# Feed-forward by one level of Strassen's scheme, with the squared hidden values passed through DRAM

## The chip, the cores and the metric

One core of a Trainium2 chip. The metric is the device time of one execution of the whole program in microseconds. Engines: TensorE (PE), VectorE (DVE), ScalarE (ACT), GpSimd (Pool), SyncE (SP, which here issues all DMAs). Fp32 data are multiplied as an upper part (rounded, type fp32r) and a lower part (the rest), three matmuls for each product of two tiles: lower x upper, upper x lower, upper x upper.

## The reference, cut to what matters

Two blocks of two layers each over x of 1024 rows (tokens) by 1024 columns: retention, latent attention, gated linear attention, and then the feed-forward that is changed here.

```python
D_FF = 4 * D_MODEL                       # 4096

def rms_norm(x, g):
    xf = x.astype(jnp.float32)
    y = xf * lax.rsqrt(jnp.mean(xf * xf, axis=-1, keepdims=True) + EPS)
    return (y * g.astype(jnp.float32)).astype(x.dtype)

def sqrelu_mlp(h, w1, w2):
    return jnp.square(jax.nn.relu(h @ w1)) @ w2
...
        x = x + sqrelu_mlp(rms_norm(x, norm_ffn), w1, w2)
    return rms_norm(x, final_norm)
```

In this program there is one such layer (DEPTH_2 = 1): x + mlp, then the final norm.

## The kernel before

The program is one stream per engine, with semaphores between them. Up to the gated linear attention nothing of it is changed. Two functions matter.

`gla_closing` (L3036) is the output product of the gated linear attention, in eight token tiles of 128 rows: 48 matmuls each (`multiply`), and 8 transposes of the gate product and 8 of the normalized residual (`transpose_x`, L3277). For tile t, DVE adds the residual (`finish`, L3208), ACT squares with a row sum (L3147), Pool forms 1/rms (L3188, L3190), DVE scales (`scale_x`, L3215), PE transposes, ACT copies the upper part (L3152), DVE subtracts for the lower part (L3219). The result is `x_upper` and `x_lower`, [128, 8, 1024] each, that is X transposed. These steps for tile t-1 lie in the stream beside the matmuls of tile t. The stages share `staging`, a buffer of two 128x1024 halves, and a function `later` puts the feed-forward's first loads and weight splits into the closing's loop. The last tile's transposes stand behind the feed-forward's first group.

`feed_forward` (L3325) runs over 8 chunks of 512 hidden columns. Chunk 0 is written out, chunks 1 to 6 are a hardware loop, chunk 7 is written out. In a chunk, `inner` (L3545) makes eight groups of 24 matmuls (8 k-tiles x 3), each the hidden values of 128 hidden columns by 512 tokens in one PSUM bank; ACT takes relu (L3424), DVE multiplies it with the value in PSUM (L3485), ACT copies the upper part to SBUF (L3429), DVE subtracts the lower (L3492). `outer` (L3561) then makes eight token tiles of 24 matmuls (4 k-tiles x 2 column halves x 3) into a pair of banks, and DVE adds each pair to an accumulator in SBUF (L3499). The accumulators start as the residual, loaded from DRAM (L3380). Weights come as 512 KB loads (L3360) through `staging`, are scaled with the norm's gain and split into upper (ACT, L3401, L3404) and lower (DVE, L3467, L3471). Pool has nothing to do here but the final norm's small operations. At the end each token tile is squared, scaled (L3504, L3529) and stored.

Of the kernel before, what the change touches and what calls it, by code (L numbers as in the profile page):

```python
# [2083 lines left out]
Closing = collections.namedtuple("Closing", "meanwhile programs split wl_done gT_mm gl_done y_mm y_done xl_done xn_done x_out")  # L2084
# [951 lines left out]
def gla_closing(place, sems, banks, xT, w, gain, x, ident, neghalf, staging, arrived, x_next, gated, gl, wb):  # L3036
# [5 lines left out]
    xh, xl = xT  # L3042
# [10 lines left out]
    xn = place("wc_xn", [P, DM], F32, 168 * KB)  # L3053
    SMALL = 198 * KB + 512 + 192
# [90 lines left out]
    def square_x(act, t):  # L3145
        act.wait_ge(y_done, t + 1)
        act.activation(xl[:, :, t * P:(t + 1) * P], y[:, t % 2, :].rearrange("p (k n) -> p k n", k=KT), ACT.Square,  # L3147
                       accum_out=sx[:, t % 2:t % 2 + 1]).then_inc(sx_done, 1)

    def x_upper(act, t, half):  # L3150
        act.wait_ge(xT_mm, 2 * t + half + 1)
        act.activation(xh[:, 4 * half:4 * half + 4, t * P:(t + 1) * P],  # L3152
                       x_ps[half][:, :].rearrange("p (k n) -> p k n", k=4), ACT.Copy).then_inc(xh_done, 1)
# [18 lines left out]
    def scalar(act, later):  # L3172
        for t in range(1, NT):
# [3 lines left out]
            later(act, t)  # L3177
            for half in range(2):
                x_upper(act, t - 1, half)
            if t + 1 < NT:  # L3180
                g_upper(act, t + 1, 1)
        square_x(act, NT - 1)

    def gpsimd(pool):
        for t in range(NT):
            u = t % 2
            pool.wait_ge(sx_done, t + 1)
            pool.tensor_scalar(mx[:, u:u + 1], sx[:, u:u + 1], 1.0 / DM, EPS, ALU.mult, ALU.add).then_inc(mx_done, 1)  # L3188
            pool.wait_ge(mx_done, t + 1)
            pool.tensor_tensor(rx[:, u:u + 1], mx[:, u:u + 1], neghalf[:], ALU.pow).then_inc(rx_done, 1)  # L3190

# [19 lines left out]
    def scale_x(dve, t):  # L3211
# [28 lines left out]
    def vector(dve, later):  # L3240
        for t in range(1, NT):
# [74 lines left out]
    def last_x(pe):  # L3316
        for half in range(2):
# [3 lines left out]
                   (sync, scalar, gpsimd, vector, tensor), (x_upper, x_lower, last_x),  # L3321
                   wl_done, gT_mm, gl_done, y_mm, y_done, xl_done, xn_done, x_out)


def feed_forward(place, sems, banks, x, xT, gain, w1, w2, g_final, neghalf, staging, arrived, out, gl, wc):  # L3325
# [4 lines left out]
    FT = HALF // P  # L3330
    xh, xl = xT
    f_ps, y_ps = banks
    w1h = [place(f"ff_w1h{n}", [P, 2, HALF], F32R, at * KB) for n, at in enumerate((72, 76, 128, 148))]
    w1l = [place(f"ff_w1l{n}", [P, 2, HALF], F32R, at * KB) for n, at in enumerate((160, 192, 144, 152))]
    hh = place("ff_hh", [P, FT, SEQ], F32R, 80 * KB)
    hl = place("ff_hl", [P, FT, SEQ], F32R, 96 * KB)
    w2h = [place(f"ff_w2h{f}", [P, DM], F32R, at * KB) for f, at in enumerate((136, 180, 64, 132))]
    w2l = [place(f"ff_w2l{f}", [P, DM], F32R, at * KB) for f, at in enumerate((140, 184, 68, 188))]
    acc = [place(f"ff_acc{t}", [P, DM], F32, at * KB) for t, at in enumerate((156, 164, 112, 116, 120, 124, 172, 176))]
    relu = place("ff_relu", [P, HALF], F32, 196 * KB)  # L3340
    SMALL = 198 * KB
    ss, ms, rms = (place("ff_" + n, [P, NT + 1], F32, SMALL + 64 * i) for i, n in enumerate(("ss", "ms", "rms")))
    raw = staging

    def sem(name):
        return sems("ff_" + name)

    raw_in = arrived
    (x_in, final_in, out_done, ss_done, ms_done, rms_done, wh_done,
     wl_done, f_mm, relu_done, sq_done, hh_done, hl_done, y_mm, y_added, fin_done) = (  # L3350
        sem(n) for n in ("x_in final_in out_done ss_done ms_done rms_done "
                         "wh_done wl_done f_mm relu_done sq_done hh_done hl_done y_mm y_added fin_done").split())
    END = NC - 1

    def load_w(sp, c, n):
        if n < 4:
            src = w1[ds(c, 1), :, 2 * n:2 * n + 2, :].rearrange("a p k n -> p (a k n)")
        else:
            src = w2[ds(c * HALF + (n - 4) * P, P), :]
        sp.dma_start(raw[:, n % 2, :], src).then_inc(raw_in[n % 2], 16)  # L3360

    def sync_later(sp, t):
        if t == 0:
            sp.wait_ge(wc.wl_done, 7)
            load_w(sp, 0, 0)
            sp.wait_ge(wc.wl_done, 8)
            load_w(sp, 0, 1)
        if t in (4, 5):
            sp.wait_ge(wl_done, t - 3)
            load_w(sp, 0, t - 2)  # L3370

    def sync(sp):
        for n in range(4, 8):
            sp.wait_ge(wl_done, n - 1)
            load_w(sp, 0, n)
        for slot in range(2):
            sp.wait_ge(wc.x_out[slot], 16 * NT // 2)
        sp.wait_ge(wc.xn_done, NT)
        for t in range(NT):
            sp.dma_start(acc[t][:, :], x[t * P:(t + 1) * P, :]).then_inc(x_in, 16)  # L3380
        with sp.Fori(1, NC) as c:
            for n in range(8):
# [393 lines left out]
```

## Time and profile before

| | before |
|---|---|
| median of 3 runs | 2540.96 us (2540.87 to 2540.98) |
| span of the profiled execution | 2538.1 us |
| PE busy | 2511.3 us, 99% |
| DVE, ACT, Pool busy | 1239.0, 923.3, 461.0 us |
| feed-forward, from its first matmul to its last | 1834.1 to 2531.7 us |
| DMA, whole run | 194.34 MB, mean 77 GB/s |

The profile is of one execution; times are from the span's start. "Busy" of PE is not its rate: matmuls are pipelined and overlap in the record. An engine's idle time counts only where the end hangs on it. "L" is a line of the kernel before.

### The profile page before, as it was taken

What the parts mean: (1) busy time and instruction counts of PE and PEld (TensorE: products, weight loads), DVE (VectorE), ACT (ScalarE), POOL (GpSimd) and SP (SyncE); (2) the same over time, 40 slices, a digit from 0 to 9 for tenths busy, and PEclk for the clock granted to TensorE, in tenths of its full rate; (3) what the DMA queues carried; (4) which work ended last, traced back from release to release, by engine and by line L of the source; (5) the groups of instructions that cost most, each with busy time, mean ns of one, the idle gap of its engine ahead of it and who ended that gap; (6) DMA issues with size and microseconds to landing.
All of it is one profiled execution on the core that took longest, in us unless ns stands there. A gap on an engine that the chain in (4) does not pass through costs nothing.

```text
span 2538.1 us, 34788 instructions
## 1 busy us (share of the span) xinstructions
PE 2511.3 (99%) x12376; PEld 2113.7 (83%) x12376; DVE 1239.0 (49%) x2573; ACT 923.3 (36%) x1848; POOL 461.0 (18%) x933
## 2 busy tenths in 40 slices
PE   8999999999999999999899999999999999999998
PEld 7888888888888988888788888888888888888887
DVE  4553634535423521577755867865443333333334
ACT  5443433424313423555544544443332122112212
POOL 3453533435000304422000000110000000000001
PEclk9999999999999999999999999999999999999999
DMA  5220311202532222222242111113331111111111
GB/s 213 79 77 20 93 39 55 68 19 92 205 116 92 80 87 65 57 60 61 98 160 100 40 62 45 48 63 126 112 132 37 47 58 50 41 50 58 36 48 75
DMA packets 76396, 194.34 MB, mean 77 GB/s; under 512 B 8560, under 2 KB 29424, under 8 KB 75504
## 3 DMA queue, kind: packets, MB, share of 16 engines
q1 hardware_dynamic: 76272, 192.69, 23.1%
q8 instruction: 77, 1.26, 0.2%
q14 instruction: 47, 0.39, 0.0%
HBM read 152.29 MB, written 36.18 MB: 74 GB/s over the span
## 4 chain that ended last, share of the span: by engine, by line
PE 95%; DVE 2%; DMA 1%; ACT 1%; issue 1%; SPq 0%; POOL 0%; DVEq 0%; POOLq 0%; ACTq 0%
PE wc_g_ps L3545 14%; PE wc_y_ps L3561 14%; PE ra_qkv_ps L1245 14%; PE gl_vr_ps L2676 7%; PE wa_y_ps L365 7%; PE ra_gate_ps L1245 7%; PE gl_j_ps L2635 3%; PE la_x_ps L1478 3%; PE wb_y_ps L3009 3%; PE wc_y_ps L3294 3%; PE la_cq_ps L1400 1%; PE la_kv_ps L1400 1%; PE at_T_ps L1967 1%; PE gl_l_ps L2702 1%; PE at_j_ps L1918 1%; PE at_v_ps L1918 1%
## 5 line engine op out<-in xcount | busy, mean ns | idle before, releaser
L3545 PE MATMUL wc_g_ps<-x_upper,ff_w1l 128*128 128x512 f32 x512 | 199.3, 389 | 0.0
L3545 PE MATMUL wc_g_ps<-x_upper,ff_w1h 128*128 128x512 f32 x512 | 199.2, 389 | 0.0
L3561 PE MATMUL wc_y_ps<-ff_w2l,ff_hh 128*128 128x512 f32 x512 | 199.2, 389 | 0.0
L3545 PE MATMUL wc_g_ps<-x_lower,ff_w1h 128*128 128x512 f32 x512 | 199.2, 389 | 0.0
L3561 PE MATMUL wc_y_ps<-ff_w2h,ff_hl 128*128 128x512 f32 x512 | 199.2, 389 | 0.0
L3561 PE MATMUL wc_y_ps<-ff_w2h,ff_hh 128*128 128x512 f32 x512 | 199.2, 389 | 0.0
L3499 DVE TENSOR_TENSOR ff_acc<-wc_y_ps,ff_acc 128x1024 f32<-128x1024 f32 x63 | 77.2, 1225 | 210.8 <-PE wc_y_ps L3561 210.8
L3424 ACT ACTIVATE ff_relu<-wc_g_ps 128x512 f32<-128x512 f32 x64 | 38.3, 599 | 378.9 <-PE wc_g_ps L3545 378.9
L3485 DVE SCALAR_TENSOR_TENSOR wc_g_ps<-wc_g_ps,ff_relu 128x512 f32<-128x512 f32 x64 | 44.8, 700 | 178.6 <-ACT ff_relu L3424 178.6
L3453 POOL TENSOR_SCALAR ff_ms<-ff_ss 128x1 f32<-128x1 f32 x8 | 1.8, 221 | 686.9 <-ACT x_lower L3441 686.0
L3545 PEld LDWEIGHTS wc_g_ps<-x_upper,ff_w1h 128*128 128x128 f32 x512 | 96.1, 188 | 20.0
L3561 PEld LDWEIGHTS wc_y_ps<-ff_w2h,ff_hh 128*128 128x128 f32 x512 | 96.1, 188 | 20.0
L3561 PEld LDWEIGHTS wc_y_ps<-ff_w2l,ff_hh 128*128 128x128 f32 x512 | 96.1, 188 | 20.0
L3545 PEld LDWEIGHTS wc_g_ps<-x_lower,ff_w1h 128*128 128x128 f32 x512 | 96.1, 188 | 20.0
L3561 PEld LDWEIGHTS wc_y_ps<-ff_w2h,ff_hl 128*128 128x128 f32 x512 | 96.1, 188 | 19.9
L3545 PEld LDWEIGHTS wc_g_ps<-x_upper,ff_w1l 128*128 128x128 f32 x512 | 96.1, 188 | 19.9
L1245 PE MATMUL ra_qkv_ps<-ra_wide_h,ra_xl 128*128 128x512 f32 x256 | 104.1, 407 | 8.5 <-DVE ra_wide_l L975 8.2
L1030 DVE TENSOR_TENSOR ra_sT<-ra_s_ps,ra_decay 128x128 f32<-128x128 f32 x64 | 18.6, 291 | 188.4 <-PE ra_s_ps L1284 188.4
L1245 PE MATMUL ra_qkv_ps<-ra_narrow_h,ra_xl 128*128 128x512 f32 x256 | 103.7, 405 | 0.0
L365 PE MATMUL wa_y_ps<-wa_wh,wa_gl 128*128 128x512 f32 x256 | 102.2, 399 | 0.8 <-DVE ra_vl L1050 0.6
L2676 PE MATMUL gl_vr_ps<-gl_vrh,x_lower 128*128 128x512 f32 x256 | 102.1, 399 | 0.0
L1245 PE MATMUL ra_qkv_ps<-ra_wide_h,ra_xh 128*128 128x512 f32 x256 | 101.0, 395 | 0.0
(460 smaller groups left out, 6995.0 us busy)
## 6 DMA issues: line engine op xcount, KB each, us to landing
staging<-in_w_ff SPq DMA_DIRECT2D x64, 512.0 KB, 3.7
ra_raw<-in_w_wide_a SPq DMA_DIRECT2D x24, 512.0 KB, 3.9
ra_raw<-in_w_narrow_a SPq DMA_DIRECT2D x16, 512.0 KB, 3.7
staging<-in_w_vr_c SPq DMA_DIRECT2D x16, 512.0 KB, 4.5
wa_gin<-gated_a SPq DMA_DIRECT2D x6, 1024.0 KB, 4.8
ra_first_raw<-in_w_wide_a SPq DMA_DIRECT2D x8, 512.0 KB, 8.1
ra_x_rows<-in_x SPq DMA_DIRECT2D x8, 512.0 KB, 5.7
gated_a<-ra_sg SPq DMA_DIRECT2D x32, 128.0 KB, 2.0
```

Source lines behind the costliest of these rows:

```text
L365: last = pe.matmul(y_ps[slot][:, c, :], a[:, slot, kt, :], b[kt][:, c * HALF:(c + 1) * HALF], start=(kt == 0 and i == 0), stop=(kt == KW - ...
L1245: last = pe.matmul(out, a[:, kt, t * P:(t + 1) * P], b[:, kt, at:at + HALF], start=(kt == 0 and i == 0), stop=(kt == KT - 1 and i == 2))
L1400: last = pe.matmul(out, xx[kt // 4][:, kt % 4, t * P:(t + 1) * P], ww[:, kt, a:b], start=(kt == 0 and i == 0), stop=(kt == KT - 1 and i == 2))
L1478: last = pe.matmul(x_ps[:, j % 2, :], a[:, kt, f % 4 * P:(f % 4 + 1) * P], b[kt // 4][:, kt % 4, half * HALF:(half + 1) * HALF], start=(kt ...
L1918: pe.matmul(out, al, bh, start=start, stop=False)
L2635: last = pe.matmul(out, w[:, r, cols], xx[:, r, at], start=(r == 0 and i == 0), stop=(r == KT - 1 and i == 2))
L2676: last = pe.matmul(vr_ps[t % 2][:, :], xx[:, r, t * P:(t + 1) * P], w[:, r, :], start=(r == 0 and i == 0), stop=(r == KT - 1 and i == 2))
L3009: last = pe.matmul(y_ps[t % 2][:, c, :], a[t % 2][:, kt, :], b[kt][:, c * HALF:(c + 1) * HALF], start=(kt == 0 and i == 0), stop=(kt == KW ...
L3294: last = pe.matmul(y_ps[t % 2][:, c, :], a[t % 2][:, kt, :], b[kt][:, c * HALF:(c + 1) * HALF], start=(kt == 0 and i == 0), stop=(kt == KW ...
L3499: dve.tensor_tensor(acc[t][:, :], y_ps[t % 2][:, :, :].rearrange("p a n -> p (a n)"), acc[t][:, :], ALU.add).then_inc(y_added, 1)
L3545: last = pe.matmul(f_ps[j % 2][:, :], a[kt // 2][:, kt % 2, f * P:(f + 1) * P], b[:, kt, half * HALF:(half + 1) * HALF], start=(kt == 0 an ...
L3561: last = pe.matmul(y_ps[t % 2][:, n, :], a[:, f, t * P:(t + 1) * P], b[f][:, n * HALF:(n + 1) * HALF], start=(f == 0 and i == 0), stop=(f ...
```

## The change

X (tokens by features) and W1 are each cut into 2 x 2 blocks: tokens into even and odd tiles of 128, features into two halves; a chunk of 512 hidden columns into two halves of 256. One level of Strassen's scheme (Winograd's form) gives the four result blocks by 7 block products in place of 8. The same is done for the second product over the chunk (hidden by output columns). Products are chained in PSUM: three open a bank pair (start=True), the other four add to a pair that stands, and between them the state is copied or added out.

- Eight banks are four pairs. First product: the 7 products use pair0, pair1, pair2, pair0, pair0, pair0, pair2; `snap` (ACT, 512 wide) copies pair0 after products 1, 4, 5 and 6; `add_square` (DVE) adds pair1 or pair2 to three of these and squares with relu; `square` does the fourth. The four squared blocks of a chunk are stored to a DRAM tensor `hidden` (8 x 4 x 128 x 1024 fp32).
- All first products of the 8 chunks run first, then all second products, which load `hidden` and W2 again, four blocks of 512 KB each and chunk.
- Weight factors: four differences of blocks on Pool per chunk (`difference_first`, `_second`, `_last`), upper part on ACT, lower on DVE, in a ring of three, two products ahead. X factors: in `gla_closing`, per pair of tiles, sums on DVE and Pool (`s1`, `s2_sum`, `s3_sum`); `s4_sum` in two 2048-wide Pool operations and the split of s2 and s4 inside the first chunk. The norm's gain moves from the weights to the scaling of X (`scale_x` with `row`).
- Second product, chunks 0 to 6: both factors of a product are split: 14 upper parts on ACT, 10 lower on DVE, 4 on Pool, and Pool makes 8 sums. Every product of 24 matmuls is two pairs, and DVE adds each pair (128x1024) to an accumulator: 14 `evict` a chunk, where before there were 8 adds. Chunk 7 is done in the plain form (`direct`).
- The hardware loop is gone: the feed-forward is written out. Semaphores of the attention are cleared (by Pool) and reused.

The diff, cut to its core:

```diff
     def scale_x(dve, t):
-        dve.tensor_scalar(xn[:, :], y[:, t % 2, :], rx[:, t % 2:t % 2 + 1], None, ALU.mult).then_inc(xn_done, 1)
+        dve.scalar_tensor_tensor(xn[:, :], y[:, t % 2, :], rx[:, t % 2:t % 2 + 1], row[:, :],
+                                 ALU.mult, ALU.mult).then_inc(xn_done, 1)
...
     def scalar(act, later):
-            later(act, t)
...
+            x_upper(act, t - 1)
             if t + 1 < NT:
                 g_upper(act, t + 1, 1)
+            if t % 2 == 0:
+                sum_upper(act, t // 2 - 1)
+        later(act)
         square_x(act, NT - 1)
...
+    def scalar_later(act):
+        act.wait_ge(wc.cleared, 1)
+        w_upper(act, 0, 0)
+        w_upper(act, 0, 1)
...
+    def gpsimd(pool):
+        sums(pool, NT // 2 - 1)
+        difference_second(pool, 0)
...
+        pool.tensor_tensor(gathered(xf.s4_sum), gathered(xf.a12[0]).bitcast(F32), xf.s2_sum[:, :, :, :],
+                           ALU.subtract).then_inc(wc.xs_done, 1)
+        pool.wait_ge(wc.xs_done, 9)
+        pool.tensor_tensor(xf.s4_sum[:, :, :], xf.s4_sum[:, :, :], xf.a12[1][:, :, :].bitcast(F32), ALU.add).then_inc(wc.xs_done, 1)
+        difference_last(pool, 0)
+        for c in range(1, NC):
+            difference_first(pool, c)
+            difference_second(pool, c)
+            difference_last(pool, c)
+        sums_first(pool, 0)
+        sums_second(pool, 0)
+        second_lower(pool, 0, 1, 1, True)
+        for c in range(END):
+            sums_last(pool, c)
+            for p in (3, 4):
+                for side in range(2):
+                    second_lower(pool, c, p, side, True)
+            if c + 1 < END:
+                sums_first(pool, c + 1)
+                sums_second(pool, c + 1)
...
+    POOL_LOWER = ((4,), (1, 3, 4))
...
+    def vector(dve):
+        w_lower(dve, 0, 1)
+        scale_x(dve, NT - 1)
+        split(dve, xf.s3[1][:, :, early], xf.s3_sum[:, :, early], xf.s3[0][:, :, early], 1)
+        w_lower(dve, 0, 2)
+        x_lower(dve, NT - 1)
+        split(dve, xf.s3[1][:, :, 3 * P:], xf.s3_sum[:, :, 3 * P:], xf.s3[0][:, :, 3 * P:], 2)
+        sum_lower(dve, NT // 2 - 1)
+        for c in range(NC):
+            for p in range(PRODUCTS):
+                if c == 0 and p == 0:
+                    continue
+                if c == 0 and p == 1:
+                    add_square(dve, c, p)
+                    split(dve, gathered(xf.s2[1]), xf.s2_sum[:, :, :, :], gathered(xf.s2[0]), 3)
+                ahead = PRODUCTS * c + p + 2
+                if ahead < PRODUCTS * NC:
+                    w_lower(dve, *divmod(ahead, PRODUCTS))
...
+        for c in range(END):
+            for p in range(PRODUCTS):
+                n = PRODUCTS * c + p
+                if n:
+                    evict(dve, *divmod(n - 1, PRODUCTS), 1)
+                ahead = divmod(n + 2, PRODUCTS)
+                second_lower(dve, *ahead, 0, False)
+                evict(dve, c, p, 0)
+                second_lower(dve, *ahead, 1, False)
...
+        def inner(c, p):
+            bank = (pair0, pair1, pair2, pair0, pair0, pair0, pair2)[p]
+            pe.wait_ge(wl_done, n + 1)
...
+            for j in range(2):
+                if p in (3, 4, 5):
+                    pe.wait_ge(snap_done, 8 * c + {3: 0, 4: 2, 5: 4}[p] + j + 1)
...
+                for kt in range(KT // 2):
+                    for i, (a, b) in enumerate(((lower, xh), (upper, xl), (upper, xh))):
+                        last = pe.matmul(bank[:, j, :], a[:, kt, j * P:(j + 1) * P], b[:, kt, :],
+                                         start=(p < 3 and kt == 0 and i == 0), stop=(kt == KT // 2 - 1 and i == 2), skip_group_check=p > 2)
...
+        def outer(c, p):
+            for pair in range(2):
+                own = p in (0, 3, 4, 5)
+                bank = ((pair1, pair3) if own else (pair0, pair2))[pair]
+                last = {2: 2, 3: 0, 4: 6, 5: 8, 6: 4}.get(p)
+                if last is not None:
+                    pe.wait_ge(ev_done, 14 * c + last + pair + 1)
```

## Rows read from the trace of the kernel before

**Rows 1.** Page: span, PE's busy time, and the chain's shares by engine.

```profile
span 2538.1 us, 34788 instructions
PE 2511.3 (99%) x12376; PEld 2113.7 (83%) x12376; DVE 1239.0 (49%) x2573; ACT 923.3 (36%) x1848; POOL 461.0 (18%) x933
...
PE 95%; DVE 2%; DMA 1%; ACT 1%; issue 1%; SPq 0%; POOL 0%; DVEq 0%; POOLq 0%; ACTq 0%
```

**Rows 2.** Stretches: limits, length, busy us (instructions), clock, DMA share, GB/s.

```profile
1834.10:1878.70 44.60, 44.60 (x202) 37.02 (x201) 18.03 (x23) 14.25 (x22) 0.74 (x2) 1.00 0.44 166
1878.70:1922.20 43.50, 43.50 (x193) 36.02 (x192) 15.26 (x17) 6.32 (x10) 0.00 (x0) 1.00 0.19 61
1922.20:2009.30 87.10, 87.10 (x386) 72.09 (x386) 31.13 (x36) 18.50 (x28) 0.00 (x0) 1.00 0.15 49
```

**Rows 3.** Groups by line and shape: busy us, mean ns | idle before, releaser.

```profile
L3499 DVE TENSOR_TENSOR ff_acc<-wc_y_ps,ff_acc 128x1024 f32<-128x1024 f32 x63 | 77.2, 1225 | 210.8 <-PE wc_y_ps L3561 210.8
L3429 ACT ACTIVATE ff_hh<-wc_g_ps 128x512 fp32r<-128x512 f32 x64 | 38.4, 600 | 48.3 <-DVE wc_g_ps L3485 48.3
L3471 DVE TENSOR_TENSOR ff_w2l<-staging,ff_w2h 128x1024 fp32r<-128x1024 f32 x32 | 39.2, 1226 | 7.9 <-ACT ff_w2h L3404 7.9
L3404 ACT ACTIVATE ff_w2h<-staging 128x1024 fp32r<-128x1024 f32 x32 | 33.7, 1052 | 0.0
L3504 DVE SCALAR_TENSOR_TENSOR ff_acc<-ff_acc,ff_rms,staging 128x1024 f32<-128x1024 f32 x7 | 8.9, 1279 | 0.0
L3523 DVE TENSOR_TENSOR ff_acc<-wc_y_ps,ff_acc 128x512 f32<-128x512 f32 x2 | 1.4, 692 | 1.1 <-PE wc_y_ps L3561 1.1
...
L1786 POOL TENSOR_TENSOR at_rl<-at_twice,at_rh 128x512 fp32r<-128x512 f32 x15 | 19.3, 1284 | 86.8 <-ACT at_rh L1676 86.8
L1780 POOL TENSOR_TENSOR gate_lower<-at_v,gate_upper 128x1024 fp32r<-128x1024 f32 x8 | 19.2, 2403 | 38.3 <-ACT gate_upper L1667 38.3
```

**Rows 4.** Timeline, first token tile's end: start us, duration us, engine, line.

```profile
1884.17 0.39 PE L3561 MATMUL wc_y_ps<-ff_w2h,ff_hl 128*128 128x512 f32 x1
...
1884.37 1.23 DVE L3499 TENSOR_TENSOR ff_acc<-wc_y_ps,ff_acc 128x1024 f32<-128x1024 f32 x1 [2.75 <-PE wc_y_ps L3561]
```

**Rows 5.** DMA issues (us to landing), and SP's timeline.

```profile
ff_acc<-x SPq DMA_DIRECT2D x8, 512.0 KB, 7.2
...
1856.37 3.93 SPq L3380 DMA_DIRECT2D ff_acc<-x  x8
```

**Rows 6.** Timeline of DVE and Pool in retention; then one line's min/median/max ns.

```profile
303.58 0.45 POOL L873 TENSOR_TENSOR ra_rot<-ra_qk,ra_cos 128x128 f32<-128x128 f32 x1 [2.44 <-ACT ra_qk L665]
303.62 0.70 DVE L998 TENSOR_TENSOR staging<-ra_oS,staging 128x256 f32<-128x256 f32 x1
303.99 0.64 POOL L874 TENSOR_TENSOR ra_rot<-ra_qk,ra_cos 128x128 f32<-128x128 f32 x1
...
L998 DVE TENSOR_TENSOR ra_sg<-ra_oS,ra_sg x32: 424/427/718, 51.1 to 592.7; 128x256 f32<-128x256 f32 x32
```

**Rows 7.** Timeline of DVE and Pool in attention.

```profile
1039.42 2.40 POOL L1780 TENSOR_TENSOR gate_lower<-at_v,gate_upper 128x1024 fp32r<-128x1024 f32 x1 [2.02 <-ACT gate_upper L1667]
...
1039.64 0.42 DVE L1855 TENSOR_TENSOR gate_lower<-at_T_ps,gate_upper 128x256 fp32r<-128x256 f32 x1
...
1040.55 1.48 DVE L1864 TENSOR_SCALAR at_prob<-at_prob,at_rinv 128x384 f32<-128x384 f32 x1
...
1044.66 0.49 DVE L1864 TENSOR_SCALAR at_prob<-at_prob,at_rinv 128x512 f32<-128x512 f32 x1
```

**Rows 8.** Timeline where the feed-forward begins (first matmul 1834.1 us).

```profile
1833.11 0.60 ACT L3152 ACTIVATE x_upper<-wc_x_ps 128x512 fp32r<-128x512 f32 x1 [2.61 <-PE wc_x_ps L3277]
...
1834.55 1.23 DVE L3208 TENSOR_TENSOR wc_y<-wc_y_ps,wc_xin 128x1024 f32<-128x1024 f32 x1
...
1837.90 0.75 DVE L3215 TENSOR_SCALAR wc_xn<-wc_y,wc_rx 128x1024 f32<-128x1024 f32 x1 [2.13 <-POOL wc_rx L3190]
...
1839.74 1.03 PE L3277 MATMUL wc_x_ps<-ident,wc_xn 128*128 128x128 f32 x8
```

More of the change, by code:

```diff
@@ L3328, in feed_forward @@
+def feed_forward(place, sems, banks, x, xf, w1, w2, g_final, neghalf, staging, hidden, out, gl, wc):
     KB = 1024
     NC = D_FF // HALF
[L3330 to L3340, printed above, removed]
+    END = NC - 1
+    PRODUCTS = 7
+    x_upper, sum_upper, sums, scale_x, x_lower, sum_lower, last_x = wc.split
+    B11, B12, B21, B22 = range(4)
@@ L3372, in sync @@
[L3372 to L3386 removed]
+            sp.wait_ge(wc.cleared, 1)
@@ new lines, in second_lower, with late_lower @@
+    def second_lower(eng, c, p, side, mine):
+        done, count = lowered(side, c, p)
+        if (p in POOL_LOWER[side]) != mine:
+            return
+        n = PRODUCTS * c + p
+        upper, lower = slots[n % 3][2 * side:2 * side + 2]
+        eng.wait_ge((ph_done, qh_done)[side], n + 1)
+        eng.tensor_tensor(lower[:, :, :], second(c, p)[side], upper[:, :, :].bitcast(F32), ALU.subtract).then_inc(done, 1)
+    def late_lower(pool, side, blk, n):
+        pool.wait_ge(late_h, n + 1)
+        upper, lower = late[side, blk]
+        pool.tensor_tensor(lower[:, :, :], (h_raw, w_raw)[side][END % 2][blk], upper[:, :, :].bitcast(F32),
+                           ALU.subtract).then_inc(late_l, 1)
@@ L3525, in vector @@
+        for half in range(2):
+            dve.wait_ge(y_mm, NT + half)
+            dst = acc[1][:, half, t // 2, :]
+            dve.tensor_tensor(dst, y_bank(t)[:, half, :], dst, ALU.add).then_inc(y_added, 1)
             if half == 0:
@@ new lines, in outer @@
+        def outer(c, p):
+            n = PRODUCTS * c + p
+            ah, al, bh, bl = slots[n % 3]
+            for side in range(2):
+                pe.wait_ge(*lowered(side, c, p))
+            for pair in range(2):
+                own = p in (0, 3, 4, 5)
+                bank = ((pair1, pair3) if own else (pair0, pair2))[pair]
+                last = {2: 2, 3: 0, 4: 6, 5: 8, 6: 4}.get(p)
+                if last is not None:
+                    pe.wait_ge(ev_done, 14 * c + last + pair + 1)
+                elif c:
+                    pe.wait_ge(ev_done, 14 * (c - 1) + (10, 12)[p] + pair + 1)
+                elif own:
+                    if pair == 0:
+                        pe.wait_ge(add_done, 6 * END + 2)
+                elif pair == 0:
+                    pe.wait_ge(snap_done, 8 * NC)
+                else:
+                    pe.wait_ge(add_done, 6 * NC)
+                for u in range(2):
+                    i = 2 * pair + u
+                    for k in range(2):
+                        for m, (a, b) in enumerate(((al, bh), (ah, bl), (ah, bh))):
+                            end = pe.matmul(bank[:, u, :], a[:, k, i * P:(i + 1) * P], b[:, k, :],
+                                            start=(p < 3 and k == 0 and m == 0), stop=(k == 1 and m == 2), skip_group_check=p > 2)
+                end.then_inc(p_mm, 1)
@@ L3682, in build @@
             x_ps = [bank("wc_x_ps0"), bank("wc_x_ps1")]
+        with ExitStack() as third:
+            ff_banks = [third.enter_context(nc.psum_tensor(f"ff_ps{i}", [P, 2, HALF], F32)) for i in range(4)]
+        xf = x_forms(place)
         wb = attention_closing(place, sems, opening_banks, xT, t["w_out_b"], x1, t["g_post_b"], ident, neghalf, staging,
```

739 lines of the change are left out of this document (524 added, 215 removed).

## The prediction

> **What bounds the kernel now.** I read the page's head and its chain of waits first: PE carries 95% of the chain and is busy for 99% of the span, so only work taken from PE, or a wait put in front of it, moves the end [rows 1]. "Busy" here is not its pace: a 128x512 matmul is recorded with 389 ns, but the next starts earlier. The table by stretches gives the pace: the 192 matmuls of one second-product pass take 43.50 us, and two further passes (384 matmuls) 87.10 us, so one costs 0.2267 us, at a granted clock of 1.00 (2.4 GHz) [rows 2]. The first stretch in it is straight-line code with 8 transposes, the third is loop code; the pace is the same, so I charge nothing for the loops being written out. The other engines have room: in the pass at 1922.2 DVE is busy 31.1 of 87.1 us and ACT 18.5.
>
> **What is removed.** Before, a chunk of 512 hidden columns has 192 + 192 matmuls, eight chunks 3072. After, a first product is 7 products x 24 = 168 per chunk (1344), the second is 168 for seven chunks (1176), and the last chunk keeps the plain form (192): 2712. So 360 go: 360 x 0.2267 = **81.6 us**. Tile shapes stay 128x128 by 128x512.
>
> One product now is 24 x 0.2267 = 5.44 us, a half of it 2.72, a chunk of seven 38.1 us. Everything that feeds a product must fit there. Prices of one operation on 128x1024 fp32 [rows 3]: ACT copy 1.05, DVE add from PSUM 1.23, DVE subtraction with both inputs in SBUF 1.23, DVE scaled two-input form 1.28, Pool 2.40. A 512-wide ACT copy from PSUM is 0.60, a 512-wide DVE add 0.69, a 512-wide Pool operation 1.28.
>
> **First product, steady state: hidden.** Per chunk ACT has 7 copies and 8 snapshots (7.4 + 4.8 = 12.2 us), DVE 7 lower parts, 6 adds and 4 squares (8.6 + 4.1 + 5.1 = 17.8), Pool 4 differences (9.6). The new tight wait is that of the fifth product on the snapshot of the fourth, same bank pair: a half is ready 2.72 us before its half-bank is wanted, DVE starts 0.20 us after PE's boundary [rows 4], ACT about the same, and 0.60 follows: 1.9 us to spare, with the weight copy ahead of it (1.05) done by then. SP's stores of hidden blocks wait behind squares, and the next chunk's loads are queued ahead of them, so nobody waits for that. Stores and loads add 32 MB; eight 512 KB loads issued within 3.93 us landed with a median of 7.2 us [rows 5], some 15 us for a chunk's 4 MB of the second product in the worst reading, with some 25 us between the release of the buffers and their first use. I cost the trip through DRAM at nothing; without that cover it would be 5 us a chunk.
>
> **A resource shared by DVE and Pool.** In retention, a Pool operation runs from 303.58 to 304.03; a DVE operation with two SBUF inputs starts at 303.62 and takes 0.70 against 0.43 for its form in most cases; it ends 0.29 after Pool, which is its 256 elements at 1.04 ns. The next Pool operation takes 0.64, not 0.45: it ends 0.31 after DVE [rows 6]. In attention a Pool operation runs from 1039.42 to 1041.82. DVE work from PSUM beside it takes its usual 0.42 (no wait), while a 384-wide SBUF scaling takes 1.48 and ends 0.21 after Pool; a wider one that starts just ahead of a Pool operation takes 0.49 [rows 7]. So these two kinds exclude each other for their whole length and take turns; a DVE operation with one input in PSUM does not take part. Scaled to 1024 elements, DVE ends 1.09 after Pool and Pool 2.28 after DVE: a turn of both is 3.37 us. The Trainium skill (SBUF — State Buffer, section "SBUF: two separate sides") says the same as a rule: the pair of ports shared by DVE and Pool is an exclusive lock and the loser blocks for the whole instruction. It speaks against this change, which puts 4 to 12 Pool operations per chunk where there were none; without it the sum below would be that of the first rival.
>
> **Second product, steady state.** Per chunk DVE evicts 14 pairs (17.2 us) and makes 10 of the 14 lower parts (12.3): 29.4 of 38.1. Pool makes 8 sums and 4 lower parts: 28.8. Alone, each fits. But Pool's 12 and DVE's 10 two-input operations exclude each other: 12 x 2.28 + 10 x 1.09 = 38.3, just over PE's 38.1, if no turn is ever lost. And DVE is in order: eviction, lower part, eviction, lower part. In products 4 to 6 of a chunk (both lower parts on DVE, Pool busy throughout with the sums) a half costs a turn, 3.37, against 2.72: DVE falls behind 0.65 a half. PE meets this where a product writes the banks of the one before (3rd after 2nd, 5th after 4th, 6th after 5th). There an eviction has 2.72 - 0.20 - 1.23 = 1.3 us of slack. Laid out with Pool 1.1 us from the end of its operation when the 4th product begins, PE waits 0.3 + 0.6 + 0.6 there, and, as DVE carries the lag into the next chunk, 1.6 before its 3rd product: 3.1 us. With Pool just finished at that moment it is 0.45 and little after. I take 2.5 us for each of the six chunks with sums for a next one: **+15 us**. Ends: 0 and 6 a chunk (36 us). A gain is excluded, since nothing here shortens a matmul.
>
> **The entry.** (1) The opening weight copy. Before, it is done in good time; now it stands after the closing's last ACT copy for tile 6, which runs 1833.11 to 1833.71 [rows 8]. ACT 1.05, then the DVE part 1.23: the first matmul moves from 1834.1 to about 1836.1: **+2.0**. (2) The closing itself: scaling with the gain row is 1.28, where 0.75 stood [rows 3, 8], and one DVE operation is added before the residual add of every second tile: **+1.0** (0 to 2). (3) The first chunk's fourth product. It needs X-sum s2 (split on DVE, 128x2048) and its weight's lower part, which DVE does after it. In us from 1834.1: PE starts at 2.0, the second product ends at 14.0 (with 8 transposes, 1.03 [rows 8]), the third at 19.4, when the fourth wants to start. DVE: residual add until 3.1, scaling until 6.5 (it waits for the square and the power), split of s3 until 8.2, weight part until 9.4, tile 7's parts until 11.4, the rest of s3 at 12.5, the s1 part blocked by Pool's third difference until 15.3, adds until 16.6. Then Pool takes 4.64 for each of its two 2048-wide operations for s4 (1.28 for 512 and 2.40 for 1024 give 2.19 ns an element). The square waits for the first, to 21.0. The split of s2 waits for the second: 25.5, then 2.2 of its own: 27.7. The weight part waits for the last difference: 31.1. So PE waits 31.1 - 19.4 = **+11.7**. Without exclusion the same queue ends at 21.2: +1.8, the lower end; upper end 16, should a further Pool operation get in.
>
> **The seam and the tail.** From first to second product, chunk 0's hidden blocks and weights are requested in the 1st and 2nd product of the last chunk and used from the 6th, 20 us later: covered. Pool's six sums then need some 14 us before the second product's lower part, wanted at 43.5 us from that chunk's start: done by 38 to 42, covered. The last chunk and the tail keep matmuls and operations: 0.
>
> **Sum.** Against the profiled span: 2538.1 - 81.6 + 2.0 + 1.0 + 11.7 + 15.0 = 2486.2. The median of the runs is 2540.96, 2.9 above the span: **2489**.
>
> **Rivals.** (A) No exclusion that matters, because the turns fall into waits that DVE has anyway: 2540.96 - 81.6 + 2.0 + 1.8 = 2463. For it: each engine alone fits, and DVE waited 210.8 us for PE around its adds before [rows 3]. Against: the blocked operations [rows 6, 7], and Pool with 28.8 of 38.1 us. 20%. (B) The lag compounds: DVE never recovers in the products with one lower part, or the loads arrive late behind Pool's slips: 6 us a chunk, 2510. 13%. (C) Slower: evictions are excluded by Pool as well (they read and write an accumulator in SBUF). Then Pool's 28.8, and DVE's 12.3 and 17.2, run one after the other: 58.3 us a chunk, 20.2 above PE, over six chunks 121: 2540.96 - 81.6 + 14.7 + 121 = 2595. The sign turns at some 11 us a chunk. Against it is the 0.42 us operation from PSUM beside Pool [rows 7]. 4%. That the change does not do what it says (matmuls not removed) has no room: the count is in the code.
>
> **How the numbers follow.** Forecast 63%, A 20%, B 13%, C 4%. The forecast's own range is 2476 to 2502. The range of 8 in 10 takes in A's point and most of B: 2462 to 2511. 0.2% (5 us) is about what a measurement of this kernel can tell from no change. Faster than 2536: all but C and a thin end of B: 95%; within 0.2%: 1%; slower 4%.
>
> **What would show each step.** 2712 matmuls of the feed-forward at 0.2267 where PE does not wait; Pool operations with DVE's two-input operations ending 1.1 us after them and stretched beyond 1.23; DVE evictions at 1.23 whatever Pool does; a PE wait of some 12 us before the 4th product of the first chunk, ended by DVE's weight part; 1 to 3 us per chunk before the 3rd, 5th and 6th products of the second stage, ended by DVE evictions. The prediction is wrong if PE runs the second stage without waits (then A), if evictions are stretched (then C), or if the matmul pace changes.

## The result, and the profile after

The changed kernel takes **2497.26 us** (median of 4 runs, 2496.68 to 2498.04) against 2540.91 in the same rounds: ratio 0.9828 [0.9815, 0.9842], 43.7 us less. The forecast was 2489 with a range of 2462 to 2511: sign and range held, and the kernel is 8 us slower than the point. The profiled execution spans 2496.2 us, 41.9 less than that of before. The page's head and chain, as in [rows 1]:

```profile
span 2496.2 us, 34303 instructions
...
PE 2439.3 (98%) x12016; PEld 2047.3 (82%) x12016; DVE 1439.2 (58%) x2608; ACT 985.2 (39%) x1862; POOL 821.6 (33%) x1064
...
PE 84%; DVE 9%; issue 4%; DMA 1%; ACT 1%; SPq 0%; POOL 0%; DVEq 0%; POOLq 0%; ACTq 0%
```

The 360 instructions are gone from PE (12376 to 12016). PE still carries the chain, but DVE has 9% of it where it had 2%. PE's waits (line, releaser: us in total, times, longest us) say where; those of the attention are left out:

```profile
PE ff_ps L4021 <- DVE ff_even L3891: 13.2, 6, 5.9
PE ff_ps L3991 <- DVE ff_w_lower L3851: 11.3, 1, 11.3
...
PE ff_ps L3991 <- issue: 2.6, 1, 2.6
...
PE ff_ps L4021 <- DVE ff_odd L3891: 2.1, 7, 0.4
```

Line numbers of the changed kernel: L3991 is `inner`, L4021 `outer`, L3891 `evict`, L3796 the second product's lower parts, L3851 the weights' lower parts, L3855 `split`, L3860 the square, L3809 and L3812 Pool's two operations for s4, L3749 the last difference behind them. The table by stretches, in the columns of [rows 2]: first the stretch that stands second there, then the whole first product, and one steady chunk of the second.

```profile
1878.70:1922.20 43.50, 43.50 (x193) 36.03 (x192) 24.00 (x23) 13.91 (x18) 10.52 (x4) 1.00 0.28 104
...
1838.20:2157.00 318.80, 307.45 (x1351) 254.20 (x1352) 174.19 (x144) 106.06 (x133) 112.90 (x43) 0.98 0.33 122
...
2258.17:2298.32 40.15, 38.66 (x169) 31.38 (x169) 36.24 (x25) 14.07 (x15) 34.73 (x13) 1.00 0.27 105
```

The first line has the pace of before, 193 matmuls in 43.50 us. So what a stage takes beyond its count of matmuls is loss. The stages are cut at the starts of their first matmuls (1838.2, 2157.3, 2446.1); one matmul of the first product still starts behind the 2157.00 of the second line.

| stage | measured us | matmuls alone | loss | forecast |
|---|---|---|---|---|
| up to the first feed-forward matmul | 1838.2, before 1834.1 | | 4.1 | 3.0 |
| first product: 56 products, 8 transposes | 319.0 | 56 x 5.44 + 1.03 = 305.7 | 13.3 | 11.7 |
| second product: 49 products | 288.8 | 49 x 5.44 = 266.6 | 22.2 | 15.0 |
| last chunk and tail | | | 0 | 0 |

The losses sum to 39.6, and 81.6 - 39.6 = 42.0, against 41.9 between the spans.

**Before the fourth product.** DVE, Pool and PE in the timeline:

```profile
1851.08 5.05 POOL L3809 TENSOR_TENSOR xf_s_sum<-xf_a_upper,xf_s_sum 128x2048 f32<-128x2048 f32 x1
...
1852.90 4.32 DVE L3860 SCALAR_TENSOR_TENSOR ff_c<-ff_c 128x1024 f32<-128x1024 f32 x1
...
1856.20 5.36 POOL L3812 TENSOR_TENSOR xf_s_sum<-xf_s_sum,xf_a_lower 128x2048 f32<-128x2048 f32 x1
...
1857.14 6.58 DVE L3855 TENSOR_TENSOR xf_s_lower<-xf_s_sum,xf_s_upper 128x2048 fp32r<-128x2048 f32 x1
...
1861.53 4.38 POOL L3749 TENSOR_TENSOR staging<-staging,ff_t 128x1024 f32<-128x1024 f32 x1
...
1863.64 4.49 DVE L3851 TENSOR_TENSOR ff_w_lower<-ff_t,ff_w_upper 128x1024 fp32r<-128x1024 f32 x2
...
1867.05 0.80 PE L3991 MATMUL ff_ps<-xf_s_upper,ff_w_lower 128*128 128x512 f32 x1 [11.32 <-DVE ff_w_lower L3851]
```

Read the ends, not the durations. Pool's first s4 operation ends at 1856.13 and the square (1.28 alone, [rows 3]) at 1857.22, 1.09 later. Pool's second ends at 1861.56, the split 2.16 later. This is the queue that the prediction wrote down.

**The clock** was in no term of the sum. Stretches at this wait, and the same at the 5.9 us wait before the third product of the second stage's first chunk (the granted clock is the third number from the end; 0.50 is 1.2 GHz):

```profile
1865.00:1867.00 2.00, 0.00 (x0) 0.00 (x0) 2.00 (x2) 0.00 (x0) 0.91 (x1) 0.50 0.00 0
1867.00:1870.00 3.00, 2.95 (x7) 2.37 (x8) 2.26 (x2) 0.00 (x0) 1.70 (x1) 0.50 0.00 0
...
1871.00:1873.00 2.00, 2.00 (x10) 1.63 (x9) 0.00 (x0) 0.60 (x1) 1.86 (x2) 1.00 0.00 0
...
2176.00:2178.00 2.00, 2.00 (x6) 1.58 (x5) 0.00 (x0) 0.00 (x0) 1.61 (x1) 0.50 1.03 406
2178.00:2180.00 2.00, 2.00 (x10) 1.63 (x10) 0.95 (x1) 0.00 (x0) 0.00 (x0) 1.00 0.16 57
```

Behind the first wait the matmuls start 0.43 us apart instead of 0.227: ten of them take from 1867.05 to 1871.17, 4.1 us in place of 2.3. That is 1.8 us on top of the 11.3. A wait is counted from the recorded end of a matmul, 0.39 after its start, and the next could have started 0.23 after it: that makes 0.2 more, and together the 13.3 of the table.

**The steady chunk.** DVE and Pool take turns:

```profile
2268.51 3.39 POOL L3765 TENSOR_TENSOR ff_v<-ff_v,ff_v 128x1024 f32<-128x1024 f32 x1
2271.86 3.40 POOL L3767 TENSOR_TENSOR ff_a<-ff_a,ff_a 128x1024 f32<-128x1024 f32 x1
...
2270.69 2.30 DVE L3796 TENSOR_TENSOR ff_p<-ff_a,ff_p 128x1024 fp32r<-128x1024 f32 x1
2272.91 1.21 DVE L3891 TENSOR_TENSOR ff_odd<-ff_ps,ff_odd 128x1024 f32<-128x1024 f32 x1
2274.04 2.29 DVE L3796 TENSOR_TENSOR ff_p<-staging,ff_p 128x1024 fp32r<-128x1024 f32 x1
...
2258.17 38.69 PE L4021 MATMUL ff_ps<-ff_p,ff_p 128*128 128x512 f32 x168 [1.46 <-DVE ff_even L3891]
2298.32 38.68 PE L4021 MATMUL ff_ps<-ff_p,ff_p 128*128 128x512 f32 x168 [1.46 <-DVE ff_even L3891]
```

A turn is 3.35 us (forecast 3.37); a lower part begun under Pool takes 2.3 in place of 1.23, and an eviction from PSUM 1.21 whatever Pool does, so rival C falls. PE's one long wait of a chunk is before its third product: 1.46, or 1.6 against the pace. Another 0.1 is lost within that product, and 0.3 within the sixth. From the third product of one chunk to that of the next it is 40.13 to 40.15 us, 2.05 above 38.1.

**The seam.** The third product of chunk 2 starts at 2258.17. Its two chunks and two products before it are 16 x 5.44 = 87.0 us of matmuls, so without loss it would start at 2157.3 + 87.0 = 2244.3, and 13.9 us are lost by then. Two steady losses make 4.1; the other 9.8 are the entry into the second stage, where the prediction had 0.

```profile
2160.07 2.33 DVE L3860 SCALAR_TENSOR_TENSOR ff_c<-ff_c 128x1024 f32<-128x1024 f32 x1
...
2161.26 3.40 POOL L3786 TENSOR_TENSOR ff_a<-ff_a,ff_u 128x1024 f32<-128x1024 f32 x1
...
2162.32 3.42 DVE L3796 TENSOR_TENSOR ff_p<-ff_a,ff_p 128x1024 fp32r<-128x1024 f32 x1
...
2165.67 1.21 DVE L3891 TENSOR_TENSOR ff_even<-ff_ps,ff_even 128x1024 f32<-128x1024 f32 x1
...
2174.18 2.05 PE L4021 MATMUL ff_ps<-ff_p,ff_p 128*128 128x512 f32 x4 [5.88 <-DVE ff_even L3891]
```

PE closes the first product at 2157.3, and DVE still has its last sums and square to do, beside lower parts stretched by Pool. Its first eviction starts at 2165.67, though PE had filled that pair at 2157.3 + 2.72 = 2160.0. PE's third product waits for the third eviction: that pair was filled at 2165.4 and the eviction starts at 2172.83. It could have started 0.2 behind PE, so it is 7.2 us late; less its slack of 1.3 (2.72 - 0.20 - 1.21), that is the wait of 5.9.

### The profile page after: what moved, and what is told of

It reads as the page before. It is cut to its first block, busy times and chain, and to the rows that moved or that the text cites. A ratio compares the mean times of both kernels' runs of the same rounds, so it can differ in the third digit from the quotient of the medians.

```text
span 2496.2 us, 34303 instructions
## 1 busy us (share of the span) xinstructions
PE 2439.3 (98%) x12016; PEld 2047.3 (82%) x12016; DVE 1439.2 (58%) x2608; ACT 985.2 (39%) x1862; POOL 821.6 (33%) x1064
## 4 chain that ended last, share of the span: by engine, by line
PE 84%; DVE 9%; issue 4%; DMA 1%; ACT 1%; SPq 0%; POOL 0%; DVEq 0%; POOLq 0%; ACTq 0%
PE ra_qkv_ps L1252 14%; PE ff_ps L3991 11%; PE gl_vr_ps L2683 7%; PE ra_gate_ps L1252 7%; PE wa_y_ps L372 6%; PE ff_ps L4021 4%; PE la_x_ps L1485 3%; PE wb_y_ps L3016 3%; PE wc_y_ps L3394 3%; DVE ff_p L3796 3%; PE gl_j_ps L2642 3%; PE ff_ps L4051 2%; DVE ff_odd L3891 1%; PE la_cq_ps L1407 1%; DVE ff_even L3891 1%
## 5 line engine op out<-in xcount | busy, mean ns | idle before, releaser
L4021 PE MATMUL ff_ps<-ff_p,ff_p 128*128 128x512 f32 x1176 | 273.5, 393 | 15.4 <-DVE ff_even L3891 13.2
L4021 PEld LDWEIGHTS ff_ps<-ff_p,ff_p 128*128 128x128 f32 x1176 | 220.6, 189 | 68.2 <-issue 18.1
L3991 PE MATMUL ff_ps<-xf_s_upper,ff_w_lower 128*128 128x512 f32 x256 | 100.5, 392 | 11.3 <-DVE ff_w_lower L3851 11.3
L1252 PE MATMUL ra_qkv_ps<-ra_wide_l,ra_xh 128*128 128x512 f32 x256 | 100.7, 394 | 0.0
L1252 PE MATMUL ra_qkv_ps<-ra_narrow_h,ra_xh 128*128 128x512 f32 x256 | 100.3, 392 | 0.0
L3991 PE MATMUL ff_ps<-xf_s_lower,ff_w_upper 128*128 128x512 f32 x256 | 100.3, 392 | 0.0
L3991 PE MATMUL ff_ps<-xf_s_upper,ff_w_upper 128*128 128x512 f32 x256 | 100.2, 391 | 0.0
L1252 PE MATMUL ra_qkv_ps<-ra_narrow_l,ra_xh 128*128 128x512 f32 x256 | 100.1, 391 | 0.0
L1252 PE MATMUL ra_gate_ps<-ra_wide_h,ra_xl 128*128 128x512 f32 x256 | 100.1, 391 | 0.0
L372 PE MATMUL wa_y_ps<-wa_wh,wa_gh 128*128 128x512 f32 x256 | 100.0, 391 | 0.0
```

Source lines behind the costliest of these rows:

```text
L372: last = pe.matmul(y_ps[slot][:, c, :], a[:, slot, kt, :], b[kt][:, c * HALF:(c + 1) * HALF], start=(kt == 0 and i == 0), stop=(kt == KW - ...
L1252: last = pe.matmul(out, a[:, kt, t * P:(t + 1) * P], b[:, kt, at:at + HALF], start=(kt == 0 and i == 0), stop=(kt == KT - 1 and i == 2))
L3991: last = pe.matmul(bank[:, j, :], a[:, kt, j * P:(j + 1) * P], b[:, kt, :], start=(p < 3 and kt == 0 and i == 0), stop=(kt == KT // 2 - 1 ...
L4021: end = pe.matmul(bank[:, u, :], a[:, k, i * P:(i + 1) * P], b[:, k, :], start=(p < 3 and k == 0 and m == 0), stop=(k == 1 and m == 2), sk ...
```

## Experiments

All medians below are of fresh runs against the kernel before in the same rounds (2540.4 to 2540.7 there). The single edits gain little beside the spread of their runs: the ratios of `e1`, `e7` and `e4` are 0.982, 0.9818 and 0.9817 with about 0.0016 to either side, against 0.9828 [0.9815, 0.9842] for the change. Their medians alone tell none of them from the changed kernel, and those of `e1`, `e4`, `e5` and `e7` lie 1.3 to 3.1 us above what was forecast. What these edits show is read from their waits; what they are worth together is timed at the end, beside the changed kernel. Spans are of one execution, for `e4`, `e5` and `e7` the fastest of four.

**Is the wait before the fourth product Pool's s4 work?** First edit (`e1`), both s4 operations moved behind what DVE owes the fourth product, and the last difference ahead of them:

```diff
         difference_second(pool, 0)
+        difference_last(pool, 0)
+        pool.wait_ge(sl_done, 3)
+        pool.wait_ge(wl_done, 4)
         pool.wait_ge(wc.y_mm, NT)
...
-        difference_last(pool, 0)
```

> Pool makes its last difference of the first chunk first, and begins the two 2048-wide operations for s4 only when DVE has split s2 and made the fourth product's weight part; nothing else moves. Theory (DVE's two-input operations and Pool's exclude each other for their whole length): the square, the split of s2 and the weight part lose about 9 us of blocking, so PE's wait before the fourth product goes from 11.3 to 2 to 3 us, and the half-speed matmuls behind it (about 1.7 us) go as well. s4 now comes later: a new wait of 3 to 5 us before the sixth product. Net 6 to 9 us less than the changed kernel: 2488 to 2491. Rival (DVE's queue is simply too long there, whatever Pool does): DVE's operations keep 4.3, 6.6 and 3.4 us, the wait stays at 11, and s4's delay comes on top: 2497 to 2502.

Measured 2494.04 (2491.2 to 2499.0), span 2491.6.

```profile
1857.78 0.50 PE L3993 MATMUL ff_ps<-xf_s_upper,ff_w_lower 128*128 128x512 f32 x1 [2.69 <-DVE ff_w_lower L3853]
...
1873.43 0.76 PE L3993 MATMUL ff_ps<-xf_s_upper,ff_w_lower 128*128 128x512 f32 x1 [4.48 <-DVE xf_s_lower L3857]
```

The wait falls from 11.3 to 2.7, so Pool's work at that point is its cause: the two s4 operations and, by the queue above, the last difference behind them, which the edit moves too. 4.5 come back before the sixth product, which needs s4. Second edit (`e7`): only the second s4 operation and the difference behind it wait.

> Of the two 2048-wide Pool operations for s4 the first stays where it is and only the second, and the last difference behind it, wait for DVE's split of s2 and weight part. Theory (each 2048-wide Pool operation blocks DVE once, by up to 4.6 us): the square is still blocked, the split of s2 and the weight part are not: PE waits 4 to 5 us before the fourth product and nothing before the sixth, since s4 is ready by then. Its two waits are 4 to 5 us in all, against 11.3 in the changed kernel and 7.2 (2.7 + 4.5) with both operations late: 6 to 8 us less than the changed kernel, 2489 to 2491, with half-speed matmuls behind the wait as after the 4.5 us one. Rival (the wait before the fourth product is made by the chain of operations on DVE whatever order Pool has, and the 2.7 us was because Pool was quite idle): 7 us or more remain, 2493 or more.

Measured 2494.06 (2491.2 to 2496.0), span 2489.4: one wait of 4.9, and 0.7 before the sixth product. DVE's square is blocked once (4.33 us), its split no longer (2.28).

**Do Pool's sums cost the second product its 22 us?** (`e2`) The sums are left out, and raw blocks stand in as factors:

```diff
-        return (..., (u2[:, :, :], v2[:, :, :]), (u1[:, :, :], v1[:, :, :]),
+        return (..., (h[3], w[B22]), (h[2], w[B11]),
...
-            sums_last(pool, c)
...
-                sums_first(pool, c + 1)
-                sums_second(pool, c + 1)
```

> Leaves out Pool's 8 sums per chunk of the second product (the factors are the raw blocks, so the output is not the reference's); the same number of copies, lower parts, evictions and matmuls stays. Theory (exclusion): DVE's lower parts return to 1.2 us, all waits of PE in the second product go: a chunk takes 38.1 instead of 40.1 us, and the seam loses most of its 10 us: 22 us less in the second product, 2475 to 2478. Rival (DVE's own load of 29 us in 38, in order, is what PE waits for): a chunk keeps 1 to 2 us of waits before the third, fifth and sixth products, the seam keeps 5 or more: 2485 to 2495.

Measured 2478.14 (2477.5 to 2478.8, two runs). DVE still makes as many lower parts and evictions. The stretch of one chunk, and DVE's groups:

```profile
2220.00:2258.10 38.10, 38.10 (x170) 31.55 (x169) 28.48 (x25) 14.10 (x15) 9.82 (x4) 1.00 0.30 111
...
L3796 DVE TENSOR_TENSOR ff_p<-ff_a,ff_p 128x1024 fp32r<-128x1024 f32 x36 | 43.7, 1215 | 0.0
```

The second product runs from 2159.9 to 2426.5 by its matmuls' starts, 266.6 us: its count times the pace. All 22.2 us, at the seam too, hang on Pool's sums, and a lower part is back at 1215 ns.

**Does it matter when the sums come?** (`e3`) The three of `sums_second` moved behind `second_lower(c + 1, 1, 1)`:

> Pool makes the last two sums of the next chunk (v2, u2) after its lower part for the next chunk's second product, not before it, so that of the six sums in a row four remain beside products 4 to 6 of a chunk. Theory (a half-product with one turn of DVE and one of Pool costs 3.35 us against 2.72, and PE waits once the lag is over 1.3 us; only the number of such halves in a row counts): four or five in a row instead of six or seven, so the wait per chunk falls from 2.05 to 0.5 to 1.2 us: 5 to 8 us less over the chunks, 2489 to 2493. Rival (the exclusive resource is full over the whole chunk, 38.0 of 38.1 us, so order does not matter): unchanged, 2496 to 2499, the waits only move to other products.

Measured 2497.09 (2495.8 to 2499.2). A chunk takes 40.4 against 40.15; the waits only move (0.65 before the third product, and 0.7 each, by the pace, within the fifth and the sixth). The theory that a burst of sums was the cost fell.

**The shared time, or DVE's queue?** (`e9`) All lower parts on DVE. Pool's 8 sums and DVE's 14 then exclude each other for 8 x 2.28 + 14 x 1.09 = 33.5 us, below 38.1.

```diff
-    POOL_LOWER = ((4,), (1, 3, 4))
+    POOL_LOWER = ((), ())
```

> All four lower parts that Pool makes per chunk go to DVE; Pool keeps its 8 sums. Sum of turns 33.5 us a chunk, DVE's own work 28 operations: 32.2 us back to back. Theory 1 (exclusive resource full): no reason for a wait is left, 38.1 us a chunk and a shorter seam: 2478 to 2484. Theory 2 (DVE's time, with 0.9 us of blocking for each lower part that meets a sum, and a lag that grows in every half-product with a turn of both): 32.2 + 8 x 1.1 = 41 us a chunk or more: 2498 to 2508.

```profile
2256.37:2297.30 40.93, 39.04 (x168) 31.21 (x169) 40.71 (x29) 14.05 (x15) 24.91 (x8) 1.00 0.27 103
```

Measured 2502.12 (2500.7 to 2504.6). The chunk takes 40.93 us and DVE is busy for 40.71 of them: what is full here is DVE's queue, its own work plus the time it is blocked. The shared resource is not: by the timeline, Pool's sums and DVE's lower parts together cover 34.3 us of the chunk. In the changed kernel it is otherwise: Pool's operations and DVE's lower parts cover 38.7 of 40.15 us, more than the 38.1 that PE needs, and DVE is busy for 36.24. So there the shared time is all but full as well, and these runs do not separate which of the two makes its 2.05 us.

With one lower part moved to DVE (`e8`, `POOL_LOWER = ((), (1, 3, 4))`):

> One lower part per chunk of the second product (the fifth product's, hidden side) goes from Pool to DVE. Taking turns costs Pool 2.28 us and DVE 1.09, so the sum of turns falls from 38.3 to 37.1 us a chunk, while DVE's own work rises from 29.4 to 30.6. Theory 1 (the exclusive resource is what is full over a chunk, as the unchanged time with spread sums suggests): a chunk falls from 40.1 by about 1.2, to 38.9; 7 us less in all: 2489 to 2491. Theory 2 (DVE's time is full: its 24 operations at 1.15 us plus 0.9 us for each lower part that meets a Pool operation make 36 us, and one more adds 1 to 2): a chunk stays at 40.1 or rises to 41: 2496 to 2503.

Measured 2509.45 (2507.6 to 2511.1), above both forecasts and worse than all fourteen on DVE, with PE waiting on `ff_even` 12.7 us in 7 waits and on `ff_odd` 6.7 in 23. A chunk takes 42.1 us and DVE is busy for 41.6 of them, so its queue is full here too. Its eleven lower parts meet eleven operations of Pool and take 2.41 us each (1.21 to 3.26), 26.5 a chunk. In `e9` fourteen meet only eight and take 1.84 each, 25.8 a chunk: the moved part adds to DVE's work and takes off little of its blocking. Of the 7.6 us between the two spans 3.1 arise ahead of the second product, in code that both share. Why the ten parts of the changed kernel take only 2.09 each is open.

**The seam** (`e4`). Pool's last sums of chunk 0 wait until DVE's third eviction is done:

```diff
+            if c == 0:
+                second_lower(pool, c, 3, 1, True)
+                pool.wait_ge(ev_done, 3)
             sums_last(pool, c)
```

> In the first chunk of the second product Pool makes the lower part of the fourth product first and then waits until DVE has evicted three pairs before its last two sums of that chunk. Theory (the seam's 5.9 us wait comes from DVE operations of 3.4, 2.3 and 2.8 us that stand behind Pool's sums, at a moment when DVE also has the last squares of the first product to do): the wait before the third product falls to 0 to 2 us, and with it the half-speed matmuls behind it; 6 to 8 us less: 2489 to 2491. Rival (the seam is DVE's backlog of squares and adds alone, or the late loads): the wait stays at 4 us or more, 2494 to 2498, and Pool's later sums may add to it.

Measured 2493.17 (2491.3 to 2496.4).

```profile
2160.28 1.23 DVE L3863 SCALAR_TENSOR_TENSOR ff_c<-ff_c 128x1024 f32<-128x1024 f32 x1
...
2161.42 1.22 DVE L3796 TENSOR_TENSOR ff_p<-ff_a,ff_p 128x1024 fp32r<-128x1024 f32 x1
...
2162.56 1.22 DVE L3894 TENSOR_TENSOR ff_even<-ff_ps,ff_even 128x1024 f32<-128x1024 f32 x1
...
2169.97 2.32 PE L4024 MATMUL ff_ps<-ff_p,ff_p 128*128 128x512 f32 x9 [1.45 <-DVE ff_even L3894]
```

The square and the lower part are back at their own times, the first eviction starts 3.1 us sooner, and the wait falls from 5.9 to 1.45. The granted clock stays at 1.00 in the stretch 2168 to 2176. The second product takes 281.8 us in place of 288.8.

**The opening** (`e5`). The upper and the lower part of the first weight are made right behind tile 6's square and scaling, ahead of its transposes' copies (`later` moved up in both loops):

> The first weight block's upper part (ACT) and lower part (DVE) are made right after tile 6 is squared and scaled, not behind ACT's last copy of tile 6. Theory (the 2.6 us before the feed-forward's first matmul are this copy and DVE's part, which Pool's difference stretches to 2.24): PE goes on without a wait, 2 to 3 us less: 2494 to 2495. Rival (PE waits there for tile 6's own lower part or for Pool's difference): the wait stays at 2 us or more, 2496 to 2498.

Measured 2496.28 (2494.9 to 2497.8). The opening wait is gone (first matmul at 1835.9, not 1838.2), but the wait at the seam is 6.5 there. By its ratio, 0.9827 [0.981, 0.9843], the kernel alone can't be told from the change.

**Joined.** `e7`, `e4` and `e5` in one kernel (`e10`), the first two without the opening (`e12`), and the changed kernel again beside them:

> The three edits together: the second of Pool's two 2048-wide operations for s4 waits for the split of s2 and the fourth product's weight part; in the second product's chunk 0 Pool's last sums come behind one lower part and DVE's third eviction; the opening weight parts are made right behind tile 6. Theory (waits are serial on TensorE, so gains add): opening wait 2.7 less, wait before the first chunk's fourth product 11.3 to 4.9 and no matmuls at half speed behind it, wait at the seam 5.9 to about 1.5 and its half-speed matmuls gone. Against the changed kernel alone, the profiled span falls by 2.7 + 6.4 + 6.8 = 16 at most: 2480 to 2484, median 2483 to 2488. Rival (the wait removed in front comes back at the next place, since Pool's queue is one chain, as the seam's wait grew from 5.9 to 6.5 when the opening wait went): not more than the best single edit, 2490 or above.

> The same without the edit of the opening: s4's second operation later and the seam's order. Theory (gains add): the opening's wait of 2.7 us stays, the other two waits as in the run with all three; 2.7 us slower than that run, median 2486 to 2490. Rival (the opening's wait only shifts DVE and Pool together with TensorE, and is given back by the following wait): within 1 us of the run with all three.

> The changed kernel as it is, on the same chip and in the same rounds as the two joined versions, to have the difference between them without a change of chip. Both theories: 2496 to 2498 median, span about 2496, waits of 11.3, 5.9 and 2.7 us before the fourth product of the first chunk, at the seam and at the opening.

| | median us (5 runs) | ratio to before |
|---|---|---|
| changed kernel again | 2498.95 (2498.45 to 2499.72) | 0.9835 [0.9822, 0.9849] |
| s4 and seam | 2487.98 (2487.07 to 2490.65) | 0.9793 [0.978, 0.9807] |
| s4, seam and opening | **2483.79** (2483.01 to 2484.16) | 0.9775 [0.9761, 0.9788] |

PE's waits in the kernel with all three:

```profile
PE ff_ps L4028 <- DVE ff_even L3898: 8.2, 6, 1.5
PE ff_ps L3998 <- DVE ff_w_lower L3858: 5.0, 1, 5.0
...
PE ff_ps L4028 <- DVE ff_odd L3898: 1.3, 4, 0.4
```

The gains add: 15.2 us below the changed kernel on the same chip, by spans 3.0 up to the first feed-forward matmul, 5.6 in the first product, 6.9 in the second. The opening is worth 4.2 between the medians of the last two, whose runs do not overlap, so it does not come back elsewhere. That is more than its wait: by the two traces the first matmul starts 2.8 us sooner, and 1.6 more are in the first product, where the clock fell behind the opening's wait with two edits and did not with three. What is left is 7.7 in the first product and 15.3 in the second, most of it the steady 2.05 a chunk.

## Why the prediction held, and where it missed

- **Matmuls removed, 81.6 us: right.** Count and pace are as forecast.
- **First product in the steady state, hidden: right.** After the fourth product of the first chunk PE waits nowhere up to the seam. The trip through DRAM is hidden as well, though the loads of `hidden` landed with a median of 8.9 us, not the 7.2 of [rows 5]: Pool waited for them twice before the first two chunks' sums, 5.3 and 2.6 us, and PE never.
- **The shared resource: right**, with the sizes read from [rows 6, 7]: 1.09 after Pool, 3.35 a turn, evictions untouched. The Trainium skill (SBUF — State Buffer, section "SBUF: two separate sides") describes the pair of ports that DVE and Pool share as an exclusive lock, with the loser blocked for the whole instruction. These rows agree with it. Rival A, which did without it, is what the run without sums shows for the second product. (Its sum left out the closing's +1.0; with it A is 2464.)
- **The fourth product, 11.7: right** (11.3), and the queue is the one written down. The 1.8 us of half-speed matmuls behind it were missed.
- **The steady chunk, 2.5: a little too high** (2.05). The wait before the third product was forecast as 1.6 and is 1.46; the 1.5 at products 4 to 6 are under 0.5. That the exclusion makes it is shown by the run without sums. The reason given first, that 12 x 2.28 + 10 x 1.09 = 38.3 just fills the shared resource, fits the 38.7 us covered; but lowering that sum to 33.5 did not lower the chunk (40.93), because the other reason, DVE's queue in order, then was full. Which of the two sets the 2.05 is not shown. Rival B (6 us a chunk) did not happen: each chunk loses the same.
- **The seam, 0: wrong, and the term that was mis-sized.** The prediction looked at loads and at Pool's sums being in time, and not at DVE, where the last squares, two lower parts and Pool's last sums meet: 9.8 us beyond the steady loss. By the pace the first chunk loses 6.0 up to its third product, 1.9 in it at half clock, and 2.3 in the rest of it, with four waits of 0.26 to 0.40.
- **The entry, 3.0: too low** (4.1, of which 2.6 are the wait that the profile puts under "issue"). The first weight's lower part was taken at 1.23, but takes 2.24, since Pool's difference L3735 lies beside it (it ends at 1837.04, the lower part at 1838.12, 1.08 later): the resource that the prediction used everywhere else. The 1.1 themselves are no more than what repetition gives: in the ten profiles here with this opening the first matmul starts between 1837.6 and 1840.2, with the changed kernel run again at 1839.6.

The forecast was low on the entry (1.1), the first product (1.6), and the seam (9.8), and high on the steady chunks (15.0 - 12.4 = 2.6): 9.9 in sum. Run time less span gave back 1.8 (2.9 forecast, 1.1 here), which leaves the 8 us; the 1.1 is small because the profiled execution was the slowest of the four. That the point came this close is in part luck: the errors are partly of opposite sign, and the largest is a term that was put at 0.

## What to carry to other kernels

Where two engines exclude each other, sum up each in-order queue with the blocked time in it; the sum over the shared resource alone passed a version whose chunk was longer (40.93 against 40.15 us). Look for the places where one stage's last work meets the next one's first on such an engine: the two spots here cost 13.3 and 9.8 us, all six steady chunks together 12.4, and letting the other engine wait there until the critical work was through won 12.5 of the 23.1 back. A wait of PE can cost more than its length, as the matmuls behind it may run at half speed.

## What had not been expected of the hardware

The granted clock fell to 0.50 (1.2 GHz) during or just behind each wait of PE of 4.1 us or more in these feed-forwards (11.3, 6.5, 5.9, 5.0, 4.9, 4.5, 4.1). Below that it differed: it stayed at 1.00 with the 2.7 of `e1` and the 1.45 of `e4`, and fell behind a wait of 2.3 and one of 1.9 in `e9`; behind the opening's wait it stayed in the changed kernel (2.6, and 3.2 when run again) and fell in the run without sums (2.8), so what decides there is open. The edit that cut the 5.9 to 1.45 won 7.0 us in its stage, more than the wait's own 4.4. First the opening of the run without sums, then the remaining wait of the joined kernel:

```profile
1839.40:1842.00 2.60, 2.58 (x6) 2.12 (x7) 2.18 (x2) 1.51 (x3) 0.20 (x2) 0.50 0.28 112
```

```profile
1859.00:1861.00 2.00, 1.96 (x5) 1.60 (x6) 2.00 (x2) 0.00 (x0) 1.89 (x1) 0.50 0.00 0
1861.00:1863.00 2.00, 2.00 (x7) 1.58 (x6) 2.00 (x1) 0.00 (x0) 2.00 (x1) 0.52 0.00 0
1863.00:1865.00 2.00, 2.00 (x10) 1.65 (x9) 2.00 (x1) 0.60 (x1) 2.00 (x2) 1.00 0.00 0
```
